# Condition vectors of a two-layer decoder: 18 of 40 half units summed on VectorE, first units in two groups, key/value products in two passes

## What is computed

```
cond = silu(c)
for l in range(2):
    sh1, sc1, g1, sh2, sc2, g2 = split(cond @ w_ada[l] + b_ada[l], 6)
    h = rms_norm(x, norm_mix[l]) * (1 + sc1) + sh1
    gq, gk, gv, ga, gr, sq, sk, sv, mix_a, mix_b = split_columns(h @ w_in[l])
    y_gla = gla_branch(...) @ w_up_gla[l]          # gated linear attention
    y_swa = swa_branch(...) @ w_up_swa[l]          # sliding-window attention
    x = x + g1 * ((sigmoid(mix_a) * y_gla + sigmoid(mix_b) * y_swa) @ w_out[l])
    h2 = rms_norm(x, norm_ffn[l]) * (1 + sc2) + sh2
    x = x + g2 * moe_ffn(h2)                       # 16 experts, two per token
```

## Time and profile before

| | |
|---|---|
| median of three runs | 1503.67 us |
| profiled execution, its time | 1502.02 us |
| its span | 1500.1 us |
| TensorE matmuls busy | 1386.9 us, 92% |
| TensorE weight loads busy | 1091.2 us, 73% |
| VectorE busy | 970.1 us, 65% |
| ScalarE busy | 720.1 us, 48% |
| TensorE in the chain of waits that ends last | 72% |
| products with the condition (L1109) | 53.6 us busy, 384 records |

### The profile page before, as it was taken

One profiled execution on the slowest core, in us unless ns is written; L12 is line 12 of the kernel. 1 busy time (PEld: TensorE's weight loads), 2 busy tenths in 40 slices (PEclk: granted clock), 3 DMA queues, 4 the chain that ended last, 5 costly groups with the idle time before them and its releaser, 6 DMA issues.

```text
span 1500.1 us, 18838 instructions
## 1 busy us (share of the span) xinstructions
PE 1386.9 (92%) x7113; PEld 1091.2 (73%) x7114; DVE 970.1 (65%) x925; ACT 720.1 (48%) x772; POOL 297.1 (20%) x263
## 2 busy tenths in 40 slices
PE   3999999999989999999959999999998899999893
PEld 1666777666677788888738787788777788888572
DVE  2426575323478899999771567632657889999293
ACT  2434354122145677776552536513325667777260
POOL 1000000000014244545320000000013425444131
PEclk9999999999999999999979999999998999999997
DMA  9666502776684899999942230131365899999365
GB/s 305 237 224 205 188 1 85 239 266 200 226 326 150 297 364 393 388 378 372 333 136 73 96 113 1 57 112 63 135 223 184 304 343 366 376 378 387 139 252 188
DMA packets 157267, 341.37 MB, mean 228 GB/s; under 512 B 17150, under 2 KB 19394, under 8 KB 157186
## 3 DMA queue, kind: packets, MB, share of 16 engines
q1 hardware_dynamic: 140018, 312.77, 57.6%
q0 software_dynamic: 17168, 27.49, 5.5%
HBM read 350.68 MB, written 23.61 MB: 250 GB/s over the span
## 4 chain that ended last, share of the span: by engine, by line
PE 72%; DVE 10%; DMA 7%; ACT 4%; DVEq 3%; issue 3%; SPq 1%; POOL 0%; POOLq 0%; ACTq 0%
PE PS L1175 14%; PE PS L1176 14%; PE PS L1177 14%; PE PS L1561 7%; PE PS L1565 7%; PE PS L1569 7%; PE PS L1109 3%; DMA ring<-in_w_ada 2%; DVE ring_parts L2150 2%; ACT reg L930 2%; PE PS L1549 2%; DMA ring<-in_w_up 2%; PE PS L1616 1%; PE PS L1574 1%; DVE ring_parts L1777 1%
## 5 line engine op out<-in xcount | busy, mean ns | idle before, releaser
L1175 PE MATMUL PS<-ring_parts 128*128 128x512 f32 (+1 forms) x704 | 276.2, 392 | 9.2 <-DVE hT_parts L1785 5.3
L2150 DVE TENSOR_TENSOR ring_parts<-ring,reg_parts 128x2048 fp32r<-128x2048 f32 x124 | 278.2, 2285 | 3.5 <-ACT reg_parts L1033 3.5
L1033 ACT ACTIVATE reg_parts<-ring 128x2048 fp32r<-128x2048 f32 x124 | 230.5, 1909 | 66.8 <-DMA ring<-in_w_down 30.1
L1777 DVE TENSOR_TENSOR ring_parts<-ring,ring_parts 128x2048 fp32r<-128x2048 f32 (+1 forms) x52 | 112.9, 2210 | 164.1 <-ACT ring_parts L851 164.0
L1175 PEld LDWEIGHTS PS<-ring_parts 128*128 128x128 f32 x704 | 132.6, 188 | 63.5 <-issue 29.3
L851 ACT ACTIVATE ring_parts<-ring 128x2048 fp32r<-128x2048 f32 (+1 forms) x52 | 93.3, 1844 | 170.9 <-DMA ring<-in_w_in 128.9
L2150 DVE TENSOR_TENSOR ring_parts<-ring,hT_parts 128x2048 fp32r<-128x2048 f32 x64 | 146.2, 2287 | 12.4 <-issue 11.9
L1177 PE MATMUL PS<-ring_parts 128*128 128x512 f32 x384 | 150.0, 391 | 0.0
L1176 PE MATMUL PS<-hT_parts,ring_parts 128*128 128x512 f32 x384 | 149.8, 390 | 0.0
L1569 PE MATMUL PS<-ring_parts,reg_parts 128*128 128x512 f32 x528 | 130.6, 390 | 0.0
L1033 ACT ACTIVATE hT_parts<-ring 128x2048 fp32r<-128x2048 f32 x64 | 119.1, 1909 | 11.1 <-DMA ring<-in_w_gate 5.7
(11 more groups left out here) (326 smaller groups left out, 2406.3 us busy)
## 6 DMA issues: line engine op xcount, KB each, us to landing
ring<-in_w_up SPq DMA_DIRECT2D x32, 2048.0 KB, 16.5
ring<-in_w_gate SPq DMA_DIRECT2D x32, 2048.0 KB, 11.5
ring<-in_w_down SPq DMA_DIRECT2D x32, 2048.0 KB, 17.5
ring<-in_w_ada SPq DMA_DIRECT2D x40, 1024.0 KB, 5.4
ring<-in_w_in SPq DMA_DIRECT2D x16, 2048.0 KB, 8.1
ring<-in_w_ada SPq DMA_DIRECT2D x4, 2048.0 KB, 19.5
ring<-in_w_out SPq DMA_DIRECT2D x4, 2048.0 KB, 8.8
ring<-in_w_up_gla SPq DMA_DIRECT2D x2, 2048.0 KB, 7.8
```

Source lines behind the costliest of these rows:

```text
L1033: act.activation(w_high[part][:, cols], ring[:, 3 * k + part, cols], ACT.Copy).then_inc(w_hi[part], 1)
L1175: pe.matmul(out_, left[0], right[0], start=first, stop=False)
L1777: tt(ring_r[:, unit_slot(n), cols], w, ring_r[:, 2 + n % 2, cols].bitcast(F32), ALU.subtract).then_inc(lo_done, 1)
L2150: tt(ring_r[:, 3 * k + part, cols], ring[:, 3 * k + part, cols], w_high[part][:, cols].bitcast(F32), ALU.subtract).then_inc(w_lo[part], 1)
```

## The change

- 9 of the 20 units after the first four are no longer multiplied on TensorE: units 4, 5, 6 of layer 0 (halves 0 to 5) and units 0, 1, 4, 5, 6, 7 of layer 1 (halves 16 to 19 and 24 to 31). `sum_half` on VectorE multiplies each of a half's four chunks by its per-partition silu(c) and adds it up in a 128x512 tile, four dependent instructions a half. `condition_columns` then adds each tile over the partitions, four matmuls a unit with one moving column.
- The places of these sums on VectorE: halves 0, 1 behind the low part of W_SQ, halves 2 to 5 behind that of W_V; in the mixing stage four behind the low part of W_UPG, four behind that of W_MB1, four behind that of W_UPS. The halves that stay on TensorE keep their places.
- In the mixing stage two loads of halves, not one, stand behind the weights' load in SyncE's queue.
- The first four units come in the order 0, 2, 1, 3, and W_KV is loaded between 2 and 1. Units 0 and 2 hold chunks 0 to 3 of shift and scale. They go through bank 6, units 1 and 3 through bank 7, each pair with its own rows, columns and scales.
- The key/value products of both layers run over chunks 0 to 3 of all four token tiles first, then over chunks 4 to 7. In layer 0 unit 3's products, the second columns and the last transpose stand between.
- The spare products: 8 instead of 22.

```diff
+    FIRST_UNITS = ((0, 2), (2, 4), (1, 3), (3, 5))
+    FIRST_BANKS = (6, 7)
...
+            for i, (u, s) in enumerate(FIRST_UNITS):
+                sp.dma_start(slot(s), w_ada[0, :, 512 * u:512 * u + 512].rearrange("(c p) n -> p c n", p=P)).then_inc(loaded[s], 16)
+                if i == 1:
+                    load(0, W_KV)
             load(0, W_SQ)
...
                 for n in range(W_MA1, W_O0):
-                    load_halves(visits(n)[:-1])
+                    load_halves(visits(n)[:-2])
                     load_after(n)
-                    load_halves(visits(n)[-1:])
+                    load_halves(visits(n)[-2:])
...
+                if j % 2 == 0 and u - 1 in summed_units(l):
+                    pe.wait_ge(ada_used, ADA_FIRST + number)
...
+                for u, made in summed.items():
+                    for i in range(4):
+                        mm = pe.matmul(PS[:, bank, ADA * i + u:ADA * i + u + 1], made[:, i * P:i * P + P], ones[:, 0:1], start=False, stop=True,
+                                       skip_group_check=True)
...
                 for t in range(NT):
-                    token_major(in_bank(Q_KV + t), t, W_KV, KVA, chunk_ready=hx_lo if t == 0 else None).then_inc(skv_ready, 1)
-                    if t % 2 == 1:
-                        own_half(t // 2)
+                    token_major(in_bank(Q_KV + t), t, W_KV, KVA, chunk_ready=hx_lo if t == 0 else None, chunks_=range(4))
+                    if t == 0 and l == 0:
+                        first_unit(3)
+                    elif t == 1 and l == 0:
+                        condition_columns(FIRST_BANKS[1], 2)
+                if l == 0:
+                    pe.wait_ge(ada_added, 2)
+                    transpose_tokens(range(7, C))
+                for t in range(NT):
+                    token_major(in_bank(Q_KV + t), t, W_KV, KVA, chunk_ready=hx_lo if t == 0 else None,
+                                chunks_=range(4, C)).then_inc(skv_ready, 1)
...
+            def sum_half(l, j):
+
+                number, u, h = first_half(l) + j, (ADA_FIRST if l == 0 else 0) + j // 2, j % 2
+                made, w = summed_units(l)[u], ada_half(number)
+                if h == 0 and u - 1 not in summed_units(l):
+                    dve.wait_ge(ada_used, ADA_FIRST + number)
+                dve.wait_ge(ada_loaded[number % 2], 16 * (number // 2 + 1))
+                for g in range(4):
+                    c_ = condw[:, 4 * h + g, COND_AT:COND_AT + 1]
+                    if h == 0 and g == 0:
+                        last = ts(made, w[:, g, :], c_, None, ALU.mult)
+                    else:
+                        dve.drain()
+                        last = stt(made, w[:, g, :], c_, made, ALU.mult, ALU.add)
+                last.then_inc(ada_used, 1)
```

More of the change, by code:

```diff
@@ L1139, in transpose_tokens, with first_unit @@
                         mm.then_inc(ht_ready, 1)
[L1141 to L1148 removed]
+                def first_unit(i):
+                    u, s = FIRST_UNITS[i]
+                    pe.wait_ge(loaded[s], 16)
+                    for h in range(2):
+                        mm = condition_products(FIRST_BANKS[i // 2], slot(s)[:, 4 * h:4 * h + 4, :], u, h, i % 2 == 0 and h == 0,
+                                                i % 2 == 1 and h == 1)
+                    mm.then_inc(ada_used, 1)
                 if l == 0:
[L1151 removed]
+                    first_unit(0)
                 else:
@@ L1789, in _ @@
                 for k in range(1, C, 2):
-                    if k + 1 < C:
+                    if k + 1 < C and not (l == 0 and k == 3):
                         hT_full(k + 1)
@@ L1795, in _ @@
                     hT_low(k - 1, k + 1)
+                    if l == 0 and k == 3:
+                        first_condition(1)
+                        dve.drain()
+                        hT_full(k + 1)
                 if l == 0:
                     split_low(1)
+                    sum_halves(0, 0, 2)
                 split_low(2)
+                if l == 0:
+                    sum_halves(0, 2, 4)
                 for i in range(2):
```

98 lines of the change are left out of this document (51 added, 47 removed).

## The result

The changed kernel took 1532.02 us (median of four runs, 1530.6 to 1539.87), the kernel before 1501.07 us beside it (1497.47 to 1505.01). Changed over before is 1.0199, with a 95% interval of 1.0170 to 1.0229. The profiled span went from 1500.1 to 1528.7 us.

What follows compares the result with a forecast made beforehand. It took TensorE, its matmuls busy 92% of the span, as the bound, except in the first 50 us, where it waits for DMA. Terms summed to +7.8 us, so 1502.02 became 1509.8, given as 1510; range 1494 to 1519 us.

Steps and rivals of the forecast that it cites:

- terms 4 and 5: TensorE waits for condition halves: layer 0's V stage +9.2 us; mixing stage's GLA and SWA output products +7.4, +5.8 us.
- Term 1: Condition products of both layers: 18 halves leave TensorE, each worth 1.21 us, together -21.8 us.
- Term 2: Condition columns of both layers: 36 one-column matmuls added on TensorE at 0.22 us each, +8.0 us.
- term 6: Behind each of the three predicted waits: a stretch of slow clock, 3 x 1.7 = +5.1 us.
- term 5: Mixing stage: TensorE waits 7.4 us for half 20 at the GLA output, 5.8 us for half 32 at the SWA output.
- Term 3: Prologue of layer 0: the new load order starts the query products at 58.8 us instead of 66.10, -4.9 us.
- rival C: The prologue gives nothing, since unit 3 lands as before and the second pass needs it: 1515 us, chance 0.13.
- Term 7: Layer 1's key/value products in two passes: waiting for chunk pairs is filled with other tokens' first chunks, -1.0 us.
- Rival A: Faster: the sums keep up and the waits of layer 0 and the mixing stage shrink to 12 us; 1494 us, chance 0.2.
- Rival D: The condition columns are cheap, -4 us: 1506 us, chance 0.1.
- Rival B: Much slower: halves take ring time, V and SWA weights land 3 us later, waits grow; 1519 us, chance 0.12.

Runs made afterwards that it cites:

- The early sums: Changed kernel with tiles as moving operands, mixing-stage sums moved into VectorE's idle time and one load of a half behind each weights' load: 1492.55 us, ratio 0.9928.
- the prologue alone: Changed kernel without the sums, all 40 halves on TensorE, loads in the old order; new unit order and two-pass key/value products kept: 1503.41 us, ratio 1.0008.
- all sums early: On top of the kernel with early mixing-stage sums: layer 0's sums earlier too, four halves instead of six, halves 4 and 5 back on TensorE: 1487.21 us.

## Why the prediction was wrong

It said slower, 1510 us, and it was 1532, above the 1519 at which its range ended. The mechanism of terms 4 and 5 was right. Two steps failed, and they make 19.0 us (10.2 and 8.8) of the error of 28.6 - 7.8 = 20.8 us.

- **Term 1** (1.21 us a half) held: eight halves gave 9.7 us between halves 21 and 32. By the Trainium skill's measure, the weight loads' share ("Trainium Kernel Development and Optimization", section Best Practices), the prediction had weighed that only 68% of this comes back. The trace does not bear that out.
- **Term 2** is the first failed step: "so I take 0.22: 36 x 0.22 = +8.0 us", with 8.6 as its upper bound. The price at full clock was right (0.235 us in the run with one-column matmuls alone). No term gave the clock a chance to fall there: term 6 tied it to waits, and here TensorE has no hole. The two calls cost 18.2 us in the changed kernel, 10.2 over the term. Alone in the kernel before they cost 17.9 us by the ranking, and 9.7 of them go when the moving operand is 128 columns wide instead of one. With the tiles as moving operands 14.6 us come back. The prediction's reason for the price, that the load of the stationary operand is what counts in so short a matmul, fits the equal times with one and with 128 columns.
- **Terms 4 and 5** held: waits of 8.7, 6.6 and 5.6 us against 9.2, 7.4 and 5.8. The early sums show the cause as argued for half 6, where only the sums' places and the number of summed halves changed: the chain of sum and load behind the low parts, not VectorE's room. For halves 20 and 32 they show it together with the order of the loads, which term 5 had in its sum as the half's later landing.
- **The missing wait** is the second failed step. Term 5 noted that half 20 stands behind 2 MB of weights and stopped at the SWA output product. The same edit, `[:-2]`, puts half 36 behind W_O1. With numbers of that kind at hand (10.7 us at 1.0 us behind) such a wait could have been drawn. It measured 7.5 us, 2.4 us of slow clock, less the 1.05 us of wait that stood there before, 8.8 us net. The run with the old order there gave back 8.9 us in this stretch and 7.5 us in the median.
- **Term 6** held in kind behind the waits: 2.5, 2.5 and 1.8 us against 1.7 each (its rows, 3.51 less 1.92, give 1.6).
- **Term 3** was right at 58 us (first query product at 58.50, drawn 58.8) and worth nothing at the end. With sums, half 6 lands at 94 to 95 us under either prologue, since the sums hang on the low part of W_SQ, which the new prologue does not bring forward (it starts at 53.95 us, and at 52.32 with the old one). The prediction carried this in its wait and so lost nothing by it, but rival C priced it wrongly: a prologue without effect would have shortened the wait by as much. Without sums, the gain was given back further on; in the profile part of it went with the place of the low clock. What part of that is chance from run to run is open.
- **Term 7** did not hold. From the first key/value product of layer 1 to the first query product the kernel before takes 14.95 us (784.83 to 799.78), the prologue alone 14.80 and the changed kernel 15.84. Two passes gave 0.2 us or cost 0.9 here, not -1.0; among the kernels with one pass this stretch goes up to 16.5 us, so the term can't be read off at all. In the changed kernel the rest of the run behind the ranking lost 0.8 us. That is small beside the scatter there (see the last section).

Rival A, with waits of 12 us, did not come: the three waits that it priced were 20.9 us. With the sums in the idle time 1492.55 us came, near its 1494, but with the columns and the order of the loads changed too. Rival D was wrong in the other direction: the columns were dearer, not cheaper. Rival B's 3 us did not come either: from issue to low part the V weights took 16.6 us (drawn 16.0) and the SWA weights 14.8 (drawn 15.3).

The kernel with all sums early beats both the kernel before and the changed one: 1487 us, 1.1% under the kernel before; with the old prologue it is as fast.

## What to carry to other kernels

Work moved to an idle engine pays only where it sits in the idle time. The same 12 sums, moved ahead of the low parts and with their loads one place forward in the queue, took 18 us of wait and the slow clock behind it out of the mixing stage. When an edit changes the place of a load in a queue, follow every stage that the loop runs through, not only the one that the edit was made for. And price short matmuls for the clock as well as for their length: here the sum over the partitions cost 18.2 us with one moving column and 3.6 us with the 512-column tile as the moving operand.

## What was unexpected of the hardware

- Runs of 12 and 24 matmuls with one moving column and a stationary operand of 128x128, back to back and with TensorE busy throughout, brought windows of 8 us with a mean granted clock of 0.57 although nothing was waited for; the same with 128 columns left it at 1.00. Either kind takes 0.235 us a matmul at full clock (0.23 to 0.24).
- Stages of identical code take some us more or less with the place where the low clock falls: the prologue alone was 4.8 us ahead at 169 us and 1.3 us ahead at 1134 us, though no wait of that length stands between.
- The stretch behind the first ranking, in which the kernels differ at most in the passes of the key/value products, took from 1050.2 to 1059.3 us over the 14 profiled executions. Each kernel has one such execution, so what of this goes with the kernel and what with the execution is open; a difference of a few us at the end is not by itself an edit's.
